# Re-ordered first loads, moved work units with filler matmuls, and head sums spread by a block matrix: a two-block transformer kernel

## The chip, the cores and the metric

The kernel runs on one core of a Trainium2 chip, as one program with its own instruction stream for each engine: TensorE (PE: matmuls), VectorE (DVE), ScalarE (ACT), GpSimd (POOL) and SyncE (SP, which here only issues DMAs). Engines meet through semaphores. The metric is the device time of the whole program in microseconds, lower is better.

## The reference

One layer of each of two blocks in float32, on 256 tokens of width 2048. Cut to what is computed:

```
mod = silu(c) @ ada_w + ada_b                       # 6 x 2048, with a table added
h = rms(x) * (1 + sc_m) + sh_m                      # block 1, mixer
xx = shift(h) - h;  x_n = h + xx * mu[n]            # six mixes: r k v w a g
r, k, v = x_r @ W_r, x_k @ W_k, x_v @ W_v
w = -softplus(-(w0 + tanh(x_w @ w1) @ w2)) - 0.5;  decay = exp(-exp(w))
a = sigmoid(a0 + (x_a @ a1) @ a2);  g = sigmoid(x_g @ g1) @ g2
kk = k * k_k, each head of 64 scaled to length 1;  k = k * (1 + (a - 1) * k_a)
y = rwkv7_scan(r, decay, k, v, -kk, kk * a)         # 32 heads of 64
y = group_norm(y) + sum(r * k * r_k) * v            # sums over each head
x = x + g_m * rms((y * g) @ w_o)
x = x + g_f * rms(conv_ffn(rms(x) * (1 + sc_f) + sh_f))   # hidden 5504
z = rms(x) @ w_in                                   # block 2: q k v g_attn, b c h g_conv
q, k = rope(rms_head(q)), rope(rms_head(k))         # 16 q heads, 4 k/v heads of 64
y1 = window_attention(q, k, v, sinks) * silu(g_attn)      # window 128, blocks of 128
y2 = b * conv3(c * h) * silu(g_conv)
x = x + [y1, y2] @ w_out
x = x + sigmoid(rms(x) @ w_gate + b) * rms(p @ w_ple)
```

## The kernel before

**Layout.** Activations lie transposed, features on the 128 partitions: 16 tiles of 128 x 256 tokens make the width of 2048. A weight unit is the 128 x 2048 slab (1 MB) that makes one output tile, in 16 matmuls. Matmuls in plain float32 (line 677 and those of the recurrence) appear in the trace as two records each. From the output projection `wo` on, each weight unit and activation is split into a rounded high part (`whi`, ScalarE, line 1227) and the rest (`wlo`, VectorE, line 1687), and a product is one matmul of high weight on both activation parts (line 700, 512 columns) and one of low weight on the high part (line 701, 256 columns).

**Loads.** SP streams the weight units through a ring of four 1 MB slots (`ring`), in the order of its program; each load waits until the unit four places ahead in the ring is used, and the loads behind it in SP's queue wait too. `RV` (line 78) is the order for projections r and v: 16 r units, then the v units with "ada" units among them. An ada unit is a row block of `ada_w`, and VectorE uses it alone, in a dot product with silu(c) over 128 x 2048 elements (`dot_into`, line 1665, `ada_ring`).

**The first stage.** SP loads x, the constants, c, the parameters, two ada blocks, the three small input matrices w1, a1, g1 of the low-rank paths, and then for each of the 16 tiles of the width a pair of ada blocks and a row block of the key matrix (`row`: 128 x 1536, four ring slots). ScalarE squares x (after silu of c), TensorE sums the squares by a matrix of ones (`rms`), ScalarE takes the root, VectorE the reciprocal (`rec`), GpSimd multiplies x by it. For tile i VectorE does two dots (`dots`) that give scale and shift, ScalarE makes h and four scaled copies, VectorE adds the shifted part (`mixes`), and TensorE adds this tile's part to 4 low-rank and 12 key outputs, held in all of PSUM. This is a loop over the contraction, so TensorE starts with tile 0 of x and not with all of h.

**The rest of the mixer.** Key tiles 12 to 15, the low-rank outputs w2 and a2, head sums of the squared keys (`sums_by_head`: stationary 64 tokens, moving a 2-column matrix that sums the two heads of a tile), r with the small triangular products and their inverse on VectorE, v with transposes of the inverse between tiles, and the recurrence in four chunks of 64 tokens. In each chunk VectorE masks eight banks of products, does some ada dots (`SCAN_DOTS`) and then copies what TensorE needs for the chunk's output. After that come eight rounds `q` of normalising: TensorE spreads the head factors over partitions (`head_spread`: stationary one broadcast column) and computes two tiles of the gate product `g2`, VectorE scales y (`y_scaled`), multiplies the bonus (`v_bonus`), GpSimd adds both, and VectorE multiplies by the gate one round later (`gated_y`), which frees the gate tile's bank.

**Attention.** In the query and key tiles of `zk` each tile's squares are summed by head into 2 columns, one root and one reciprocal are taken for all ten tiles at the end, and in the gate tiles `zg` TensorE spreads two tiles' factors at a time (`two_heads`), which VectorE multiplies in. `scores`, the softmax and `pv` then run between the tiles of `zc`.

The order of the work is written out by hand in each engine's program; nothing plans it.

## Time and profile before

| | |
|---|---|
| median of 3 runs | 2066.36 us (2059.53 to 2067.49) |
| the profiled execution | 2064.75 us, its span 2063.1 us |
| busy share of the span | PE 95%, PEld 83%, DVE 67%, ACT 43%, POOL 6% |
| matmul records | 13392 |
| mean granted TensorE clock | 0.975 of full speed |
| DMA | 419.34 MB, mean 203 GB/s |

The span runs from the first to the last instruction. PE is the matmul, PEld the weight load that runs beside it. Busy shares are averages over stages with different limits. In a timeline row, "[idle before <-releaser]" says how long the engine stood idle and whose end let it go; "issue" is idle time for which the profile shows no wait. PEclk is the clock granted to TensorE, 1.00 for 2.4 GHz and 0.50 for 1.2 GHz.

### The profile page before, as it was taken

How to read it: one execution, taken by the hardware profiler on the slowest of the kernel's cores; microseconds unless marked ns; L12 is line 12 of the kernel's file. 1: busy time of each engine (PE TensorE's matmuls, PEld its weight loads, DVE VectorE, ACT ScalarE, POOL GpSimd, SP SyncE). 2: the span in 40 equal slices, each digit the busy share in tenths (PEclk: the TensorE clock that was granted, in tenths of full speed). 3: DMA queues.
4: the chain of work that ended last, by engine and by line, in shares of the span. 5: the costliest groups of instructions: out<-in, count | busy, mean ns of one | idle time of the engine just before them, and what ended most of it. 6: DMA issues, size and time to landing. Idle time of an engine off the chain costs nothing.

```text
span 2063.1 us, 34272 instructions
## 1 busy us (share of the span) xinstructions
PE 1958.8 (95%) x13392; PEld 1703.7 (83%) x13392; DVE 1389.0 (67%) x1981; ACT 897.1 (43%) x1457; POOL 121.3 (6%) x119
## 2 busy tenths in 40 slices
PE   3999999898898988999999999999989999999999
PEld 2888888787786866888888888888878888888887
DVE  5986459643765987777777776444466567767876
ACT  2335321022233545555555555444454435535553
POOL 2000001100002310000000000000010000001200
PEclk8999999999999988999999999999999999999999
DMA  9986224565743954545555556555536444445553
GB/s 403 400 352 215 102 86 160 223 258 232 288 166 125 425 205 163 183 183 183 187 184 193 186 186 221 191 184 194 191 106 241 164 163 177 150 152 216 184 184 123
DMA packets 59078, 419.34 MB, mean 203 GB/s; under 512 B 6560, under 2 KB 6688, under 8 KB 12448
## 3 DMA queue, kind: packets, MB, share of 16 engines
q1 hardware_dynamic: 54656, 384.34, 50.3%
q0 software_dynamic: 3888, 27.26, 3.3%
q10 hardware_dynamic: 432, 6.29, 0.7%
q8 instruction: 74, 1.21, 0.2%
q14 instruction: 28, 0.23, 0.0%
HBM read 411.58 MB, written 6.29 MB: 203 GB/s over the span
## 4 chain that ended last, share of the span: by engine, by line
PE 91%; DVE 4%; DMA 2%; issue 1%; ACT 1%; SPq 0%; POOL 0%; DVEq 0%; ACTq 0%
PE ps L700 41%; PE ps L701 21%; PE ps L677 12%; PE ps L781 4%; PE ps L775 1%; PE ps L761 1%; DMA ring<-in_wv 1%; PE ps L752 1%; DMA bk<-in_ada 1%; PE ps L1007 1%; PE ps L1066 1%; PE ps L797 1%; DVE ring L1665 1%; PE ps L934 1%; PE ps L664 0%
## 5 line engine op out<-in xcount | busy, mean ns | idle before, releaser
L700 PE MATMUL ps<-x_pair,whi 128*128 128x512 f32 x2464 | 881.8, 402 | 14.4 <-DVE x_pair L1721 9.9
L701 PE MATMUL ps<-x_pair,wlo 128*128 128x256 f32 x2464 | 693.8, 282 | 0.0
L1687 DVE TENSOR_TENSOR wlo<-ring,whi 128x1024 fp32r<-128x1024 f32 x468 | 547.6, 1206 | 102.9 <-ACT whi L1227 96.5
L700 PEld LDWEIGHTS ps<-x_pair,whi 128*128 128x128 f32 x2464 | 465.2, 189 | 135.0 <-issue 21.9
L1227 ACT ACTIVATE whi<-ring 128x1024 fp32r<-128x1024 f32 x468 | 462.4, 1031 | 96.4 <-PE ps L701 93.8
L701 PEld LDWEIGHTS ps<-x_pair,wlo 128*128 128x128 f32 x2464 | 467.9, 190 | 0.3
L1234 ACT ACTIVATE px<-ps 128x256 f32<-128x256 f32 x202 | 77.8, 385 | 475.0 <-PE ps L701 475.0
L700 PE MATMUL ps<-hid_pair,whi 128*128 128x512 f32 x688 | 238.8, 394 | 0.0
L701 PE MATMUL ps<-hid_pair,wlo 128*128 128x256 f32 x688 | 190.6, 277 | 0.0
L677 PE MATMUL ps<-mixb,ring 128*128 128x256 f32 x640 | 146.6, 391 | 13.6 <-DMA ring<-in_wv 12.0
L700 PEld LDWEIGHTS ps<-hid_pair,whi 128*128 128x128 f32 x688 | 129.0, 188 | 30.2 <-DVE wlo L1687 0.3
L1665 DVE CUSTOM_DVE_ANT_0 ring<-ring,cb,prm 128x2048 f32<-128x2048 f32 x42 | 97.6, 2351 | 82.1 <-DMA ring<-in_ada 81.3
L677 PEld LDWEIGHTS ps<-mixb,ring 128*128 128x128 f32 x640 | 124.8, 196 | 33.0 <-DMA ring<-in_wv 13.1
L701 PEld LDWEIGHTS ps<-hid_pair,wlo 128*128 128x128 f32 x688 | 129.2, 188 | 0.0
L677 PE MATMUL ps<-mixa,ring 128*128 128x256 f32 x512 | 116.0, 390 | 0.0
L677 PEld LDWEIGHTS ps<-mixa,ring 128*128 128x128 f32 x512 | 99.8, 196 | 14.6 <-issue 0.2
L1750 DVE TENSOR_TENSOR px<-ps,px 128x256 f32<-128x256 f32 x68 | 28.9, 424 | 119.5 <-ACT px L1234 119.2
L1695 DVE TENSOR_TENSOR px<-ps,px 128x256 f32<-128x256 f32 x134 | 56.4, 421 | 72.1 <-ACT px L1234 71.8
L2004 DVE SCALAR_TENSOR_TENSOR tmp<-px,prm,tmp 128x255 f32<-128x255 f32 x86 | 41.6, 484 | 81.5 <-ACT tmp L1480 81.5
L700 PE MATMUL ps<-y_pair,whi 128*128 128x512 f32 x256 | 89.0, 392 | 2.5 <-DVE h L1931 1.4
L781 PE MATMUL ps<-mixb,ring 128*128 128x256 f32 x384 | 86.3, 382 | 0.0
L1480 ACT ACTIVATE tmp<-px,prm 128x256 f32<-128x256 f32 x86 | 51.8, 602 | 70.4 <-DVE px L1695 70.4
(291 smaller groups left out, 2286.3 us busy)
## 6 DMA issues: line engine op xcount, KB each, us to landing
ring<-in_fi SPq DMA_DIRECT2D x86, 1024.0 KB, 4.8
ring<-in_zin SPq DMA_DIRECT2D x52, 1024.0 KB, 4.8
ring<-in_ada SPq DMA_DIRECT2D x42, 1024.0 KB, 6.9
ring<-in_fo SPq DMA_DIRECT2D x32, 1024.0 KB, 4.8
bk<-in_ada SPq DMA_DIRECT2D x22, 1024.0 KB, 10.3
ring<-in_wr SPq DMA_DIRECT2D x16, 1024.0 KB, 4.8
ring<-in_wv SPq DMA_DIRECT2D x16, 1024.0 KB, 4.9
ring<-in_wo SPq DMA_DIRECT2D x16, 1024.0 KB, 8.9
```

The source lines that it names most:

```text
L677: last = mm(ps[0:m, bank, 0:S], w[:, k * m:(k + 1) * m], act[:, k, :], start=k == 0, stop=k == n - 1)
L700: mm(ps[:, bank, 0:2 * S], w_h, pair_k, start=first and k == 0, stop=False)
L701: m = mm(ps[:, bank, 0:S], w_l, pair_k[:, 0, :], start=False, stop=last and k == n - 1)
L781: last = mm(outer_bank(m), ring[:, i % RING, m * P:(m + 1) * P], mixb[:, i, :], start=i == 0 and m % 2 == 0, stop=i == NT - 1, skip_group_ ...
L1227: A(whi[:, hf % WB, 0:m], ring[:, u % RING, 1024 * x:1024 * x + m], ACT.Copy).then_inc(w_hi, 1)
L1234: A(part[:, (TILE[name] + k) % 4, :], ps[:, (TILE[name] + k) % BANKS, S:2 * S], ACT.Copy).then_inc(x_part, 1)
L1480: A(tmp[:, (k % 4) * S:(k % 4 + 1) * S], join_in("fi", k, it), ACT.Identity, scale=param_at("fcw", 4 * FT, kk), bias=param_at("fcb", 0, kk ...
L1665: V.tensor_tensor_reduce(out=w, in0=w, in1=cb[:], scale=1.0, scalar=prm[:, m:m + 1], op0=ALU.mult, op1=ALU.add, accum_out=mod[:, m:m + 1]) ...
L1687: V.tensor_tensor(wlo[:, hf % WB, 0:m], ring[:, u % RING, 1024 * x:1024 * x + m], whi[:, hf % WB, 0:m].bitcast(F32), ALU.subtract).then_in ...
L1695: return V.tensor_tensor(o, ps[:, (TILE[name] + k) % BANKS, 0:S], o, ALU.add).then_inc(joined, 1)
L1750: own(V.tensor_tensor(o, ps[:, (TILE[name] + k) % BANKS, 0:S], o, ALU.add))
L2004: own(V.scalar_tensor_tensor(d[:, 1:S], b[:, 0:S - 1], param_at("fcw", 2 * FT, kk), d[:, 1:S], ALU.mult, ALU.add))
```

## The change

1. First loads: x, then only the first 773 columns of the constants (the rest comes after the first stage, waited for by `ld_late`), c, parameters. The low-rank input matrices are no longer loaded ahead; their rows are appended to the key matrix's row blocks, 1984 columns instead of 1536. ScalarE squares x before it takes silu of c; VectorE takes the reciprocal before its first dots, and does tile i - 1's mixes between tile i's two dots.
2. `RV`: v0 to v5 without ada units, then two before each v tile and two behind the last. 22 dots before the recurrence instead of 24, and 4, 6, 6, 4 in its chunks instead of 5, 5, 4, 4.
3. `all_sums_by_head`: stationary 128 tokens of a tile, moving 2 columns, for two of the three uses. For it the a/r buffer `ar` is laid out tile, a/r, token, where it was tile, chunk, a/r, token.
4. `gated_y(q)` in round q.
5. `keep_clock`: n matmuls of the identity on a 256-column constant, into a bank that nothing reads: 10 and 18 around the second sum of squares (between `wo` and the FFN), 8 before `zk`.
6. Attention: the squares of a query or key tile times a block matrix of ones (`blk`) give head sums that are already spread; root on ScalarE (`head_root`), reciprocal and product on VectorE (`normalized`) for each tile. `pv` uses the first keys for both query blocks in one matmul of 256 columns. The softmax's small buffers lie over `omu`.

SP's queue at projections r and v, before and then after. in_wr and in_wv are the r and v units, in_ada the dot units:

```order
L465 DMA ring<-in_wr 128x2048 x16
L465 DMA ring<-in_wv 128x2048 x3
L465 DMA ring<-in_ada 128x2048
L465 DMA ring<-in_wv 128x2048
L465 DMA ring<-in_ada 128x2048
L465 DMA ring<-in_wv 128x2048
```

```order
L468 DMA ring<-in_wr 128x2048 x16
L468 DMA ring<-in_wv 128x2048 x6
L468 DMA ring<-in_ada 128x2048 x2
L468 DMA ring<-in_wv 128x2048
L468 DMA ring<-in_ada 128x2048 x2
```

Three more v units stand ahead of the first dot unit, and dot units then come in pairs.

VectorE's first instructions, before and then after. ISA rows are the dots and the reading of their sum, RECIPROCAL is that of the root of x's mean square, sc the scale of one tile, the rows on ar, sg and mixb the four mixes:

```order
L1771 TENSOR_TENSOR prm<-prm 128x96
L1665 ISA bk,mod<-bk,cb,prm 128x2048
L1665 ISA mod 128x1
L1665 ISA bk,mod<-bk,cb,prm 128x2048
L1665 ISA mod 128x1
L1779 SCALAR_TENSOR_TENSOR sc<-mod,prm 128x1
L1727 RECIPROCAL tmp<-tmp 128x256
L1665 ISA bk,mod<-bk,cb,prm 128x2048
```

```order
L1774 TENSOR_TENSOR prm<-prm 128x96
L1730 RECIPROCAL tmp<-tmp 128x256
L1668 ISA bk,mod<-bk,cb,prm 128x2048
L1668 ISA mod 128x1
L1668 ISA bk,mod<-bk,cb,prm 128x2048
L1668 ISA mod 128x1
L1785 SCALAR_TENSOR_TENSOR sc<-mod,prm 128x1
L1668 ISA bk,mod<-bk,cb,prm 128x2048
L1668 ISA mod 128x1
L1793 SCALAR_TENSOR_TENSOR ar<-h,prm,ar 128x255 x2
```

The reciprocal moved ahead of the first two dots, and the first mixes stand after three dots instead of four.

VectorE in the first rounds of the head normalisation, before and then after. The rows on h from ar are `y_scaled`, those on mixa `v_bonus`, those on h from h and ps `gated_y`:

```order
L1923 SCALAR_TENSOR_TENSOR h<-ar,prm,ps 128x256 x2
L1917 TENSOR_TENSOR mixa<-mixa,ps 128x512
L1923 SCALAR_TENSOR_TENSOR h<-ar,prm,ps 128x256 x2
L1917 TENSOR_TENSOR mixa<-mixa,ps 128x512
L1931 TENSOR_TENSOR h<-h,ps 128x256 x2
```

```order
L1928 SCALAR_TENSOR_TENSOR h<-ar,prm,ps 128x256 x2
L1922 TENSOR_TENSOR mixa<-mixa,ps 128x512
L1936 TENSOR_TENSOR h<-h,ps 128x256 x2
L1928 SCALAR_TENSOR_TENSOR h<-ar,prm,ps 128x256 x2
L1922 TENSOR_TENSOR mixa<-mixa,ps 128x512
```

The gate product moved up by one round, so VectorE reaches it with GpSimd's addition of the same round still to come.

The diff, cut to its core:

```diff
-    RV += [("v", _k)] + [("ada", len(RV) - NT - _k + _j) for _j in range(0 if _k < 2 else 1 if _k < 8 else 3 if _k < 10 else 2)]
-SCAN_DOTS = (5, 5, 4, 4)
-RV += [("ada", 24 + _k) for _k in range(sum(SCAN_DOTS))]
+    RV += [("v", _k)] + [("ada", len(RV) - NT - _k + _j) for _j in range(0 if _k < 5 else 2)]
+RING_DOTS = len(RV) - 2 * NT
+SCAN_DOTS = (4, 6, 6, 4)
+RV += [("ada", RING_DOTS + _k) for _k in range(sum(SCAN_DOTS))]
...
+ROW = KO * P + 2 * LORA + 2 * P
...
+    put("blk", (i // HD == j // HD).astype(np.float32))
...
-        ar = ar_f.rearrange("p (i c a t) -> p i c a t", i=NT, c=NCH, a=2)
+        ar = ar_f.rearrange("p (i a c t) -> p i c a t", i=NT, c=NCH, a=2)
+        ar_i = ar_f.rearrange("p (i a s) -> p i a s", i=NT, a=2)
...
-            sp.dma_start(cst[:], t["const"]).then_inc(ld_par, 16)
+            sp.dma_start(cst[:, 0:EARLY], t["const"][:, 0:EARLY]).then_inc(ld_cst, 16)
...
-                sp.dma_start(ring[:, i % RING, 0:KO * P], t["wkr"][i]).then_inc(ld_row[i % RING], 16)
+                sp.dma_start(ring[:, i % RING, 0:ROW], t["wkr"][i]).then_inc(ld_row[i % RING], 16)
             ada_pair(0)
-            sp.dma_start(lora_w1, t["w1"]).then_inc(ld_lora, 16)
-            sp.dma_start(lora_a1, t["a1"]).then_inc(ld_lora, 16)
-            for k in range(2):
-                sp.dma_start(flat_c[:, 2048 * k:2048 * (k + 1)], t["g1"][k]).then_inc(ld_lora, 16)
             row(0)
             for i in range(1, NT):
                 ada_pair(i)
                 row(i)
+            sp.dma_start(cst[:, EARLY:], t["const"][:, EARLY:]).then_inc(ld_late, 16)
...
+            def keep_clock(n, bank):
+                for _ in range(n):
+                    mm(ps[:, bank, 0:S], ident, const("smask"), start=True, stop=True)
...
+            def all_sums_by_head(src, bank):
+                for tt in range(TT):
+                    for i in range(NT):
+                        m = mm(ps[:, bank, tt * NH + 2 * i:tt * NH + 2 * i + 2], src(i)[:, tt * P:(tt + 1) * P], const("blk2"),
+                               start=True, stop=True)
...
-            hidden = [("w", lora_w1, LORA), ("a", lora_a1, LORA), ("g", flat_c[:, 0:2048], P), ("g", flat_c[:, 2048:4096], P)]
+            hidden = [("w", KO * P, LORA), ("a", KO * P + LORA, LORA), ("g", ROW - 2 * P, P), ("g", ROW - P, P)]
             for i in range(NT):
                 pe.wait_ge(mix_b, 4 * (i + 1))
-                for n, (name, w, m) in enumerate(hidden):
-                    last = mm(ps[0:m, n // 2, (n % 2) * S:(n % 2 + 1) * S], w[:, i * m:(i + 1) * m], mix_slot(name, i),
+                pe.wait_ge(ld_row[i % RING], 16 * (i // RING + 1))
+                for n, (name, o, m) in enumerate(hidden):
+                    last = mm(ps[0:m, n // 2, (n % 2) * S:(n % 2 + 1) * S], ring[:, i % RING, o:o + m], mix_slot(name, i),
                               start=i == 0 and n % 2 == 0, stop=i == NT - 1, skip_group_check=True)
                     if i == NT - 1:
                         last.then_inc(pe_step, 1)
-                pe.wait_ge(ld_row[i % RING], 16 * (i // RING + 1))
                 for m in range(KO):
                     last = mm(outer_bank(m), ring[:, i % RING, m * P:(m + 1) * P], mixb[:, i, :],
...
-            for c in range(NCH):
-                m = sums_by_head(c, lambda i: ar[:, i, c, 1, :], 4)
-            m.then_inc(hs_sum, 1)
+            all_sums_by_head(lambda i: ar_i[:, i, 1, :], 4).then_inc(hs_sum, 1)
...
-                    for c in range(NCH):
-                        m = sums_by_head(c, lambda i: rkr[:, i, c * CH:(c + 1) * CH], 4)
-                    m.then_inc(bon_sum, 1)
+                    all_sums_by_head(lambda i: rkr[:, i, :], 4).then_inc(bon_sum, 1)
...
             rms(1, None, NT)
+            keep_clock(10, 6)
             rms(2, mixb)
+            keep_clock(18, 6)
...
-                    m = head_sums(e)
-                    if e == 9:
-                        m.then_inc(at["sum"], 1)
+                    if e >= 2:
+                        pe.wait_ge(at["root"], e - 1)
+                    mm(ps[:, 4 + e % 2, 0:S], const("blk"), qsq[:, e, :], start=True, stop=True).then_inc(at["sum"], 1)
...
+            keep_clock(8, (TILE["zk"] + 3) % BANKS)
...
+                    pe.wait_ge(at["root"], 10)
...
-                    if e >= 2:
-                        pe.wait_ge(at["nrm"], e - 1)
-                    for tt in range(TT):
-                        m = spread_pair(rs, tt * 32 + 2 * e, 4 + e % 2, tt * P)
-                    m.then_inc(at["bc"], 1)
...
-                mm(o[:, 0:P], vtok[:, 0, kv:kv + HD], p[:, 0:P], start=True, stop=True)
-                mm(o[:, P:S], vtok[:, 0, kv:kv + HD], p[:, P:2 * P], start=True, stop=False)
-                mm(o[:, P:S], vtok[:, 1, kv:kv + HD], p[:, 2 * P:3 * P], start=False, stop=True).then_inc(at["pv"], 1)
+                mm(o[:, 0:S], vtok[:, 0, kv:kv + HD], p[:, 0:2 * P], start=True, stop=False, skip_group_check=True)
+                mm(o[:, P:S], vtok[:, 1, kv:kv + HD], p[:, 2 * P:3 * P], start=False, stop=True,
+                   skip_group_check=True).then_inc(at["pv"], 1)
...
                     one(k, None, k == n - 1)
+            act.wait_ge(ld_x, 16)
+            squares(0, mixa)
             act.wait_ge(ld_c, 16)
             A(cb[:], cb[:], ACT.Silu).then_inc(silu_c, 1)
-            act.wait_ge(ld_par, 32)
-            act.wait_ge(ld_x, 16)
-            squares(0, mixa)
...
+            def head_root(e):
+                act.wait_ge(at["sum"], e + 1)
+                A(qsq[:, e, :], ps[:, 4 + e % 2, 0:S], ACT.Sqrt, scale=1.0 / HD, bias=const("eps")[:, 0:1]).then_inc(at["root"], 1)
...
-                if k == 11:
-                    act.wait_ge(at["sum"], 1)
-                    A(rt[:].rearrange("p (a n) -> p a n", a=2)[:, :, 0:20],
-                      ps[:, 4, 0:64].rearrange("p (a n) -> p a n", a=2)[:, :, 0:20], ACT.Sqrt, scale=1.0 / HD,
-                      bias=const("eps")[:, 0:1]).then_inc(at["root"], 1)
+                for e in new_heads(k - 1):
+                    head_root(e)
...
                 for j in range(2):
                     s, m = i % 3 * 2 + j, i + NT * (1 - j)
                     dve.wait_ge(ld_ada[0][s], 16 * (i // 3 + 1))
                     dot_into(m, ada_slot(0, s))
+                    if j == 0 and i:
+                        mixes(i - 1)
...
+            rec(0)
             dve.wait_ge(silu_c, 1)
-            dots(0)
-            rec(0)
-            for i in range(1, NT):
+            for i in range(NT):
                 dots(i)
-                mixes(i - 1)
             mixes(NT - 1)
+            dve.wait_ge(ld_cst, 16)
...
-                if q in (4, 6):
-                    y_lo_part((q - 4) // 2)
+                gated_y(q)
+                if q in (2, 4, 6):
+                    y_lo_part(q // 2 - 1)
                 if q == 5:
                     lo_part("wo", 0)
-            gated_y(7)
-            y_lo_part(2)
             y_lo_part(3)
             for k in range(NT):
                 lo_part("wo", k + 1) if k < NT - 1 else lo_part("fi", 0)
...
+            def normalized(e):
+                dve.wait_ge(at["root"], e + 1)
+                own(V.reciprocal(qsq[:, e, :], qsq[:, e, :]))
+                dve.wait_ge(at["rot"], e + 1)
+                V.tensor_tensor(qk[:, e, :], qk[:, e, :], qsq[:, e, :], ALU.mult).then_inc(at["nrm"], 1)
...
-                if k == 11:
-                    dve.wait_ge(at["root"], 1)
-                    V.reciprocal(rs[:].rearrange("p (a n) -> p a n", a=2)[:, :, 0:20],
-                                 rt[:].rearrange("p (a n) -> p a n", a=2)[:, :, 0:20]).then_inc(at["rec"], 1)
...
+                if k >= 8:
+                    normalized(k - 8)
...
-                for e in two_heads(k):
-                    dve.wait_ge(at["bc"], e + 1)
-                    dve.wait_ge(at["rot"], 10)
-                    V.tensor_tensor(qk[:, e, :], qk[:, e, :], ps[:, 4 + e % 2, 0:S], ALU.mult).then_inc(at["nrm"], 1)
+                if k < 6:
+                    normalized(4 + k)
```

## Rows read from the trace of the kernel before

**Rows 1.** Page, part 4: the chain that ended last, by engine.

```profile
PE 91%; DVE 4%; DMA 2%; issue 1%; ACT 1%; SPq 0%; POOL 0%; DVEq 0%; ACTq 0%
```

**Rows 2.** TensorE's waits: what waited, on what; us in all, count, longest.

```profile
PE ps L677 <- DMA ring<-in_wv: 12.0, 4, 7.0
```

**Rows 3.** DMA issues, 0 to 170 us: size, median us from issue to landing.

```profile
mixa<-in_x SPq DMA_DIRECT2D x1, 2048.0 KB, 7.9
```

**Rows 4.** Timeline, start: start us, busy us, engine, line, operation, shape, count.

```profile
16.24 9.81 PE L664 MATMUL ps<-mixb,cst 128*128 128x256 f32 x32 [16.24 <-ACT mixb L1196]
26.60 1.75 DVE L1727 RECIPROCAL tmp<-tmp 128x256 f32<-128x256 f32 x1 [4.79 <-ACT tmp L1202]
28.44 14.09 POOL L571 TENSOR_TENSOR mixa<-mixa,tmp 128x512 f32<-128x512 f32 x8 [27.85 <-DVE tmp L1727]
...
32.31 3.20 DVE L1665 CUSTOM_DVE_ANT_0 bk<-bk,cb,prm 128x2048 f32<-128x2048 f32 x1 [3.95 <-DMA bk<-in_ada]
...
43.75 1.99 PE L775 MATMUL ps<-ar 128*96 128x256 f32 x4 [17.69 <-DVE mixb L1787]
...
156.88 27.79 PE L677 MATMUL ps<-mixb,ring 128*128 128x256 f32 x128
```

**Rows 5.** Page, part 5: costliest groups | busy, mean ns | idle before.

```profile
L1687 DVE TENSOR_TENSOR wlo<-ring,whi 128x1024 fp32r<-128x1024 f32 x468 | 547.6, 1206 | 102.9 <-ACT whi L1227 96.5
...
L1665 DVE CUSTOM_DVE_ANT_0 ring<-ring,cb,prm 128x2048 f32<-128x2048 f32 x42 | 97.6, 2351 | 82.1 <-DMA ring<-in_ada 81.3
```

**Rows 6.** Windows: PE, PEld, DVE, ACT, POOL busy (records), PEclk, DMA share, GB/s.

```profile
100.00:110.00 10.00, 10.00 (x48) 8.60 (x47) 8.95 (x14) 3.41 (x8) 0.00 (x0) 1.00 1.01 427
```

**Rows 7.** Timeline, PE, value projection.

```profile
390.51 15.64 PE L677 MATMUL ps<-mixb,ring 128*128 128x256 f32 x64 [6.97 <-DMA ring<-in_wv]
...
511.47 7.17 PE L677 MATMUL ps<-mixb,ring 128*128 128x256 f32 x32 [2.97 <-DMA ring<-in_wv]
```

**Rows 8.** Windows, PE alone, inside the key's head sums.

```profile
200.00:202.00 2.00, 2.00 (x44) 1.00 0.86 348
```

**Rows 9.** Timeline, PE: the key's head sums, and sums in an attention tile.

```profile
198.49 9.31 PE L761 MATMUL ps<-cst,ar 128*64 128x2 f32 x128
207.72 9.66 PE L677 MATMUL ps<-mixa,ring 128*128 128x256 f32 x32
...
1600.49 0.50 PE L1051 MATMUL ps<-cst,qsq 128*128 128x2 f32 x4
1600.86 0.68 PE L1090 MATMUL ps<-qk,cst 128*128 128x256 f32 x2
```

**Rows 10.** Timeline, PE, the recurrence's first chunk.

```profile
537.74 3.31 PE L984 MATMUL ps<-cum,zb 128*64 128x64 f32 x64 [2.80 <-DVE cum L1896]
```

**Rows 11.** Timeline, head normalisation rounds.

```profile
628.37 0.87 DVE L1923 SCALAR_TENSOR_TENSOR h<-ar,prm,ps 128x256 f32<-128x256 f32 x2 [2.06 <-PE ps L752]
...
643.17 1.28 POOL L599 TENSOR_TENSOR h<-h,mixa 128x512 f32<-128x512 f32 x1 [3.74 <-DVE h L1923]
643.70 0.74 DVE L1931 TENSOR_TENSOR h<-h,ps 128x256 f32<-128x256 f32 x2
644.26 1.97 PE L1007 MATMUL ps<-sg,ring 128*128 128x256 f32 x8 [1.21 <-DVE h L1931]
...
664.58 2.44 DVE L1935 TENSOR_TENSOR y_pair<-h,y_pair 128x1024 fp32r<-128x1024 f32 x2
```

**Rows 12.** Windows, PE alone, the FFN's first matmuls.

```profile
784.00:786.00 2.00, 2.00 (x7) 0.50 0.57 246
```

**Rows 13.** Timeline, ACT: outputs of two plain and two gate tiles.

```profile
1613.55 0.39 ACT L1234 ACTIVATE px<-ps 128x256 f32<-128x256 f32 x1 [3.67 <-PE ps L701]
1619.16 0.38 ACT L1234 ACTIVATE px<-ps 128x256 f32<-128x256 f32 x1 [3.02 <-PE ps L701]
...
1632.06 0.39 ACT L1234 ACTIVATE px<-ps 128x256 f32<-128x256 f32 x1 [4.29 <-PE ps L701]
1638.92 0.39 ACT L1234 ACTIVATE px<-ps 128x256 f32<-128x256 f32 x1 [4.28 <-PE ps L701]
```

76 lines of the change are left out of this document (35 added, 41 removed).

## The prediction, made before the changed kernel ran

> **What bounds the kernel now.** I read the chain of waits by engine first [rows 1]. It lies on TensorE for 91% of the span, so an edit pays only where it shortens TensorE's own work or closes a stretch in which TensorE stands still. Next I read what TensorE waits for [rows 2]: four waits on value weights, 12.0 us, are one entry, and the timeline shows them and the rest in place. The start comes first: TensorE's first tile of the first product stage begins only at 43.75 us and the stage ends at 156.88 [rows 4]. Sixteen steps in 113.1 us, the first at half clock, make 6.91 us a step. While they run the DMA engines are full too, share 1.01 at 427 GB/s [rows 6]. So this stage has two limits a few per cent apart. Later come gaps behind a transfer [rows 7], behind VectorE in the recurrence [rows 10] and in the head normalisation [rows 11], and half-clock stretches after longer pauses [rows 12].
>
> **The start.** Before, x, all constants, c and the parameters (2.10 + 0.85 + 1.05 + 0.47 = 4.47 MB) land before ScalarE squares x. Now only x is needed, the first load of all. It lands 7.9 us after its issue [rows 3], at about 9, and a quarter of the squares later, 1 us, the ones-matmuls that begin at 16.24 can begin: near 10.3. From them to GpSimd's first multiply before is 28.44 - 16.24 = 12.2 us [rows 4]; that puts GpSimd at 22.5. All of this 6 us does not reach TensorE. Before, VectorE did its first two 2.35 us dot products [rows 5] while TensorE summed. Now the reciprocal stands ahead of them in VectorE's order and they follow at 22.4, beside GpSimd's eight multiplies. Those two do not overlap: a dot takes 3.20 us while GpSimd works, and GpSimd's eight multiplies take 14.09 us [rows 4], though an operation of their shape takes 1.28 [rows 11], eight 10.2. Serial work up to the first finished mix: three dots 7.0, four mixes and the small scale 1.9, seven or eight multiplies 9.2. That is 18.3 from 22.4, so TensorE starts at 40.9 instead of 43.75, a gain of 2.8 us. The ends are -1 (a ninth slot lost, x later) and +8 (no serialising at all).
>
> The Trainium skill, "SBUF — State Buffer", section "SBUF: two separate sides", says that VectorE and GpSimd hold one port pair by an exclusive lock and the loser blocks for a whole instruction. The trace agrees: 3.20 us against 2.35. By free overlap the gain would be 8, not 2.8.
>
> Each row load grows from 1536 to 1984 columns, so a step moves 2.10 + 1.02 = 3.11 MB, 7.3 us at 427 GB/s [rows 6], against 6.91 for TensorE. The row loads run up to four steps ahead, and 0.4 us a step over the 11 steps that reuse the ring costs 4.5 us of that lead, which is about 16 (three steps less the 4.5 us of a load). I price it at nothing. VectorE's step (two dots and four mixes) keeps its length.
>
> **The value projection.** Value tile 5 waits 6.97 us and starts at half clock: two projections take 15.64 us [rows 7] where four take 27.79 [rows 4], so 1.8 more. Its load stood in SP's queue behind dot units that VectorE could not yet consume. Now values 0 to 5 come before any dot unit, and TensorE has work for those 7 us. Two more of the four waits are 12.0 - 6.97 - 2.97 = 2.06 [rows 2, 7], behind three dot units in a row; now there are never more than two, and filler work stands behind those tiles. The last wait, 2.97, stays: the same two dot units stand ahead of value 15. Gain 6.97 + 1.8 + 2.06 = 10.8. The ends are 0 (rival B) and 12.
>
> **Sums by head.** Two places go from 128 records of 64 stationary columns to 64 records of 128. In the clear stretch 44 narrow ones start in 2 us, 0.045 each [rows 8], so 128 are 5.8 us; the stretch takes 9.31 because its clock falls to half, and the next projection takes 9.66 instead of 6.93 for the same reason [rows 9]. A wide one (L1051) takes 0.37 us for four, 0.092 each or more [rows 9], so 64 are 5.9. I take nothing for both places together. If they are 0.11 and the clock falls as before they lose 1 to 1.5 each; if the clock holds, they give 3 and the slow projection's 2.7 back. Ends -3 and +11.
>
> The Trainium skill, "TensorE: Matmul & The Clock Gate", section "LDWEIGHTS (loading the stationary operand)", says a load's time goes by its columns, not its rows, so half the loads of double width gain nothing. The trace agrees, 0.045 against 0.092. By a fixed price per load the two places would gain 4.6 and 4.4, and the sum would be 9 us larger (rival A).
>
> **Recurrence dots.** Chunk 0 loses one dot of five; TensorE waited 2.80 there for the copy behind them [rows 10], so 2.35 of it goes. Chunks 1 and 2 gain one and two dots in front of their copy. Before, the copy came after the matmuls in both, so most of 2.35 and 4.7 lies in VectorE's pause; I charge 0.4 in all. Gain 1.9. Ends -3 and 2.8.
>
> **Head normalisation.** TensorE waits about 1.2 us in each round [rows 11], for a gating product that VectorE does one round after its input. The gate now stands in its own round, so VectorE waits for GpSimd's 1.28 us instead (0.6 of it under the bonus product), but the gate tiles of the next round find their bank free. A VectorE round is the scaling 0.87, the bonus product and the gate of about 0.74 each and 0.6 left of GpSimd's, 3.0 us [rows 11], plus 1.2 in every other one and 2.35 in round 5. TensorE's is 5.0 less 1.2, 3.8. So TensorE stops waiting up to round 5, then VectorE leads to the last low half, which now ends at 664.58 + 2.44 = 667.0. Counting from the first scaling at 628.37: five rounds of 3.8, then 5.2, 4.05, 2.85, and 2.4 for the last high and low halves are 33.5, so 661.9. (Rounds 2, 4 and 6 carry a low half of 1.2.) Gain 5.2. Ends 2 and 8.
>
> **Fillers.** Ahead of the FFN the clock is at 0.50, its 1.2 GHz level, when the split matmuls start [rows 12], and ahead of the attention projections likewise. A pair of 512 and 256 columns is 0.64 us there and 0.32 at 2.4 GHz. The ten fillers before the sum of squares let its last quarter run at full speed: 0.6 us. The 18 before the FFN keep the clock for its first half tile, but the second half waits for the split input either way: 0.5. The 8 before the attention projections end before its input is there, and its first eight pairs then take 2.6 instead of 5.1 us; a later wait on GpSimd's sums takes some of it: 2.0. Sum 3.1. Ends -2 (a filler stands in front of real work, or the clock falls in the rest of the pause) and 4.
>
> **Attention heads.** The spread of the normaliser leaves TensorE's gate tiles. A gate tile with two spreads takes 1638.92 - 1632.06 = 6.86 us, a plain one 1619.16 - 1613.55 = 5.61 [rows 13]. Five times 1.25 is 6.3. In the query/key tiles the wide ones-block matmul (two records, about 0.43) replaces four records at 0.37 [rows 9]: ten times 0.06, nothing to speak of. VectorE gets ten reciprocals of 1.75 us [rows 4] and a product each. A gate tile has two low halves of 1.2 [rows 5] and two short products, 3.1 us, and gets 2.2 more: 5.3 of 5.6. A query/key tile has three short products besides, 4.3, and comes to 6.5 in a tile of 5.61 + 0.37 + 0.43 = 6.4. It fits by a hair, and only the last four of those tiles have it; besides, the next low halves are wanted only after the tile that runs. If it slips, scores wait for the tenth head: up to 3. First keys for both query blocks: the same columns in fewer instructions, nothing; ends -1 and 2. Gain 6.3, ends 3 and 7.
>
> **Everything else** (the attention buffers put over the mix coefficients, the other layout of the a/r buffer, the late rest of the constants) has no duration that could change by these rows: the same elements per instruction. Ends -2 and 2.
>
> **Sum.** 2.8 + 10.8 + 0 + 1.9 + 5.2 + 3.1 + 6.3 = 30.1 us. The profiled execution took 2064.75 (span 2063.1 and 1.65 around it), 1.6 under the median of the runs, 2066.36. 2064.75 - 30.1 = 2034.7; I say 2035.
>
> **Rivals.**
> A. The sums by head get shorter in proportion and the clock stays up behind them: 9 us more, 2026. For it: half the instructions. Against it: 0.092 for a wide one [rows 9].
> B. The value gap only moves. After every value tile two dot units and the next value have to be loaded, and where nothing stands between two projections that costs 2.97 us [rows 7]. If tiles 7 to 10 meet it because VectorE frees its slots late, four times 2.97 is 11.9: 2047. Against it: sums and transposes stand between most of those tiles.
> C. Slower. The first stage goes over to the DMA queues: with 3.11 MB a step they decide as soon as a step takes longer than 6.91 us for more steps than the lead covers. To turn the sum round it needs about 9.4 us a step, 331 GB/s; then 16 steps cost 40 us and the time is about 2075. For it: share 1.01 already, nothing in reserve [rows 6]. Against it: 427 GB/s over the same queue and even longer rows.
> D. The stalls that go are taken back one for one by VectorE, which gets the reciprocals, the later dots and the wait for GpSimd: no change, 2062.
>
> **How the numbers follow.** My forecast 0.61, A 0.14, B 0.17, C 0.04, D 0.04. About 0.5%, 10 us, is what a measurement of this kernel can tell from no change. Forecast, A and B are all faster by more, except for a small part of B: faster 0.91. D and that part: 0.05. C: 0.04. The ends of the costs above, taken as independent, spread by about 12 us each way, so the range is 2022 to 2049; it holds A and B. The likeliest case alone has 2028 to 2043.
>
> **What would show it.** TensorE's first tile at 40 to 42 us and dots of over 3 us behind the reciprocal; steps of 6.9 us with no transfer wait. No wait on value weights above 1 us but the 2.97 at tile 15. 64 records of the head sums in 6 to 9.5 us each. No VectorE wait inside the normalisation rounds up to round 5, and the first split output tile near 655 less the shift. Full clock at the start of FFN and attention. Gate tiles of 5.6 to 5.7 us. It is wrong if TensorE waits for VectorE in the gate tiles, if the steps of the first stage take over 7.2 us, or if value tiles 7 to 10 wait.

## The result, and the profile after

The changed kernel takes 2044.70 us, median of 4 runs (2028.08 to 2045.49); the kernel before, with one run more on the same chip, 2064.42 (2059.53 to 2067.49). The ratio is 0.9884, 95% interval 0.9853 to 0.9916: faster by 1.2%. I forecast 2035, in 2022 to 2049. The profiled execution took 2044.51 us (span 2042.6), so the two profiles differ by 20.2 us where my sum had 30.1.

What TensorE waits for (line that waited, what let it go: us in all, times, longest), one row of the kernel before and then four of after, against [rows 2]:

```profile
PE ps L973 <- issue: 4.1, 3, 1.6
```

```profile
PE ps L680 <- DMA ring<-in_wv: 3.4, 2, 3.0
PE ps L984 <- issue: 5.7, 3, 2.1
PE ps L680 <- issue: 3.1, 1, 3.1
PE ps L703 <- DVE y_pair L1940: 3.7, 1, 3.7
```

The 12.0 us for value weights fell to 3.4. What grew has no releaser ("issue": the profile shows nothing that TensorE waits for). Such stops were there before too: four in the recurrence, 5.5 us in all, against five and 7.6 us after, and one inside value tile 14, 1.58 us against 3.14. And the wait inside `wo`'s first tile, 1.13 us before, is 3.71.

The start, timeline of after, against [rows 4]:

```profile
9.88 9.54 PE L667 MATMUL ps<-mixb,cst 128*128 128x256 f32 x32 [9.88 <-ACT mixb L1197]
21.38 1.75 DVE L1730 RECIPROCAL tmp<-tmp 128x256 f32<-128x256 f32 x1 [7.66 <-ACT tmp L1203]
23.17 3.45 DVE L1668 CUSTOM_DVE_ANT_0 bk<-bk,cb,prm 128x2048 f32<-128x2048 f32 x1
23.22 16.49 POOL L574 TENSOR_TENSOR mixa<-mixa,tmp 128x512 f32<-128x512 f32 x8 [22.63 <-DVE tmp L1730]
...
40.04 2.02 PE L791 MATMUL ps<-ar,ring 128*96 128x256 f32 x4 [20.62 <-DVE mixb L1793]
```

TensorE starts its first tile at 40.04 instead of 43.75, and GpSimd's eight multiplies now take 16.49 us instead of 14.09: three dots and four mixes of VectorE lie beside them, and not two dots and two mixes.

One more thing changed here, on ScalarE. Before it takes the root it loads another function table, 1.28 us. The row before, and then after:

```profile
18.96 1.28 ACT L1202 ACT_TABLE_LOAD   x1
```

```profile
19.51 1.28 ACT L1203 ACT_TABLE_LOAD   x1 [3.72 <-PE ps L667]
```

Before, this load lay beside TensorE's sums, and the root began at 26.10, as the sums ended at 26.05. Now silu stands between the squares and the root, the load waits for the sums, which end at 19.42, and the root begins at 20.80. So about 1.3 us of the earlier x are lost there, and no run took them back.

The value projection, timeline of TensorE, against [rows 7]:

```profile
345.42 48.51 PE L680 MATMUL ps<-mixb,ring 128*128 128x256 f32 x224
...
471.75 4.24 PE L897 MATMUL ps<-h,cum 64*32 64x32 f32 x256
...
479.98 16.17 PE L680 MATMUL ps<-mixb,ring 128*128 128x256 f32 x61 [3.14 <-issue]
...
499.12 8.86 PE L680 MATMUL ps<-mixb,ring 128*128 128x256 f32 x32 [2.97 <-DMA ring<-in_wv]
```

Seven projections run in one piece: the gap of 6.97 us is gone. But three records into value tile 14 TensorE stops for 3.14 us, and the 61 records behind the stop take 16.17 us. The kernel before, around value tiles 13 and 14:

```profile
477.13 3.14 PE L875 MATMUL ps<-cum,h 64*64 64x32 f32 x84 [1.52 <-issue]
...
496.79 11.71 PE L677 MATMUL ps<-mixb,ring 128*128 128x256 f32 x53 [1.58 <-issue]
```

There the stop in tile 14 was 1.58 us and the rest of the two projections ran at full clock. After, TensorE in the stop and behind it (us, busy (records), PEclk, DMA share, GB/s):

```profile
476.00:480.00 4.00, 0.86 (x4) 0.87 1.02 420
480.00:484.00 4.00, 4.00 (x10) 0.50 0.23 94
```

From the start of value tile 14 to the recurrence it is 32.58 us instead of 26.59 (from 475.92 and 492.57), 6.0 us lost: the longer stop, half clock behind it, and half clock behind the wait at tile 15. Ahead of tile 14 other things got shorter: the stop of 1.52 us at 477.13 became one of 0.31 and value tile 13 behind it ran at full clock, 2.8 us together, and the two small waits for value weights gave 1.7.

A round of the head normalisation and the second half of `wo`'s first tile, against [rows 11]:

```profile
624.28 0.75 DVE L1936 TENSOR_TENSOR h<-h,ps 128x256 f32<-128x256 f32 x2 [0.70 <-POOL h L602]
625.84 0.87 DVE L1928 SCALAR_TENSOR_TENSOR h<-ar,prm,ps 128x256 f32<-128x256 f32 x2 [0.81 <-PE ps L755]
626.72 0.69 DVE L1922 TENSOR_TENSOR mixa<-mixa,ps 128x512 f32<-128x512 f32 x1
```

```profile
645.54 0.49 PE L703 MATMUL ps<-y_pair,whi 128*128 128x512 f32 x1 [1.51 <-DVE h L1936]
652.29 0.49 PE L703 MATMUL ps<-y_pair,whi 128*128 128x512 f32 x1 [3.71 <-DVE y_pair L1940]
```

VectorE is now the one that waits in a round (0.70 and 0.81 us), and the rounds start 3.82 us apart.

The ledger below is made of the start of the same instruction in both traces. Its last column is the difference within the stretch.

| stretch | before | after | gained |
|---|---|---|---|
| to the key's head sums | 198.49 | 194.79 | 3.7 |
| key's head sums and the next projection | 18.83 | 19.11 | -0.3 |
| value projection up to the bonus sums | 57.24 | 48.34 | 8.9 |
| bonus sums and two projections | 25.79 | 25.98 | -0.2 |
| from there to the recurrence | 87.29 | 88.76 | -1.5 |
| recurrence | 106.15 | 106.64 | -0.5 |
| normalisation to the second half of `wo`'s first tile | 41.85 | 37.15 | 4.7 |
| from there to `wo`'s first output | 3.07 | 4.64 | -1.6 |
| last `wo` output to second FFN output | 44.58 | 43.63 | 0.9 |
| FFN output matrix, 15 tiles | 223.60 | 227.89 | -4.3 |
| last FFN output to first `zk` output | 28.33 | 25.78 | 2.6 |
| the rest of the `zk` tiles | 79.11 | 79.90 | -0.8 |
| gate tiles 0 to 7 | 46.99 | 40.99 | 6.0 |
| the last 34 outputs (`zo` and `pg`) | 194.17 | 191.58 | 2.6 |
| what is left: fi and `zc` | 687.80 | 687.65 | 0.2 |

The rows come to 20.5, the difference of the spans. Two of them belong to no edit: in the FFN's output matrix and in the last projections the same matmuls run at another pace.

### The profile page after: what moved, and what is told of

The parts are those of the page before. It is cut to its first block, busy times and chain, and to the rows that moved or that the text cites. A ratio compares the mean times of both kernels' runs of the same rounds, so it can differ in the third digit from the quotient of the medians.

```text
span 2042.6 us, 33937 instructions
## 1 busy us (share of the span) xinstructions
PE 1967.2 (96%) x13204; PEld 1710.0 (84%) x13204; DVE 1409.8 (69%) x1990; ACT 902.8 (44%) x1467; POOL 124.5 (6%) x119
## 4 chain that ended last, share of the span: by engine, by line
PE 90%; DVE 5%; issue 2%; DMA 2%; ACT 1%; POOL 1%; SPq 0%; DVEq 0%; POOLq 0%; ACTq 0%
PE ps L703 42%; PE ps L704 21%; PE ps L680 12%; PE ps L796 4%; PE ps L791 1%; DVE ring L1668 1%; PE ps L776 1%; DMA ring<-in_wv 1%; PE ps L812 1%; PE ps L1073 1%; PE ps L667 1%; PE ps L769 1%; POOL h L602 0%; DVE bk L1668 0%; DVE mixb L1895 0%
## 5 line engine op out<-in xcount | busy, mean ns | idle before, releaser
L703 PE MATMUL ps<-hid_pair,whi 128*128 128x512 f32 x688 | 243.3, 399 | 0.0
L703 PEld LDWEIGHTS ps<-hid_pair,whi 128*128 128x128 f32 x688 | 129.3, 188 | 32.4 <-DVE wlo L1690 0.3
L2006 DVE SCALAR_TENSOR_TENSOR tmp<-px,prm,tmp 128x255 f32<-128x255 f32 x86 | 41.6, 484 | 81.5 <-ACT tmp L1482 81.5
```

Source lines behind the costliest of these rows:

```text
L703: mm(ps[:, bank, 0:2 * S], w_h, pair_k, start=first and k == 0, stop=False)
L2006: own(V.scalar_tensor_tensor(d[:, 1:S], b[:, 0:S - 1], param_at("fcw", 2 * FT, kk), d[:, 1:S], ALU.mult, ALU.add))
```

## The pace of a matmul pair, and why runs differ

Outputs of the FFN's output matrix (43 pairs of a 512 and a 256 column matmul in each tile), after, and then the same kernel in another execution:

```profile
1304.44 0.38 ACT L1235 ACTIVATE px<-ps 128x256 f32<-128x256 f32 x1 [2.13 <-PE ps L704]
1319.62 0.39 ACT L1235 ACTIVATE px<-ps 128x256 f32<-128x256 f32 x1 [2.11 <-PE ps L704]
```

```profile
1294.26 0.39 ACT L1235 ACTIVATE px<-ps 128x256 f32<-128x256 f32 x1 [2.04 <-PE ps L704]
1309.16 0.38 ACT L1235 ACTIVATE px<-ps 128x256 f32<-128x256 f32 x1 [2.04 <-PE ps L704]
```

15.18 us a tile, and 14.90: 353 and 347 ns a pair, at granted clock 1.00 in both. The second is from this experiment, which changes nothing:

> The changed kernel once more, unchanged, to learn what differs between executions. Its four times were 2044.5, 2045.5, 2028.1 and 2044.9 us, and in its profiled execution TensorE takes 5.55 us for a tile of the output projection wo, 5.65 for one of the FFN's fi, 15.19 for one of fo, 5.55 for most of the last projection zo; the kernel before had 5.55, 5.65, 14.91 and 5.65, with the same matmuls and no waits. Theory P (the pace of a matmul pair takes one of two values, 347 or 353 ns, by execution and not by code): the times again spread over more than 8 us with values near both 2028 and 2045, and this profile can show other paces in fi, fo or zo than the first one, at unchanged start (TensorE's first tile at 40.0 +-0.5 us). Theory Q (the pace belongs to the program's code): the same paces stage by stage, 5.55, 5.65, 15.19, 5.55, and the one time of 2028 stays alone.

Measured: 2041.50 us, median of 6 (2032.44 to 2045.66), ratio 0.990 [0.9883, 0.9916] to 17 runs of the kernel before. In its profile fi's tiles take 5.55 us (5.65 in the first profile of the same kernel), fo's 14.91 (15.19), and the last projections begin at 5.55 and end at 5.65; the first tile starts at 40.73, 0.2 past the bound I had set. Theory P holds: two values and nothing between them. Over the fourteen profiles each of `wo`, fi and fo shows both (`wo` 5.55 or 5.65), and within the last projections the pace can change behind a tile that took 0.4 us longer. fi alone has 85 intervals, 9 us between the two, fo 16 tiles, 4.5. The profiles of after and of its repeat are 12.1 us apart, and these two stages alone make 13 of it. The four runs of the changed kernel spread over 17 us; the ones without a trace cannot be split up like this, so that the pace explains their spread too is likely and not shown. What selects the pace is open. For the experiments it means that a stretch of the trace decides, and the whole time only over several runs.

## The experiments

**Dots ahead of the reciprocal.**

```diff
-            rec(0)
             dve.wait_ge(silu_c, 1)
-            for i in range(NT):
+            dots(0)
+            rec(0)
+            for i in range(1, NT):
                 dots(i)
```

> The changed kernel with VectorE's first two dots ahead of the first reciprocal again, as in the kernel before; all else of the new start stays. Theory S (VectorE and GpSimd take turns, so dots done before GpSimd starts are not lengthened and don't lengthen GpSimd's eight multiplies): the two dots run at about 15.9 to 20.6 us at 2.35 each, the reciprocal still at 21.4, GpSimd at 23.2, and behind the reciprocal only one dot of about 3.4 and four mixes stand before TensorE's first tile: 23.2 + 3.4 + 5.8 = 32.4, against 40.0. The first stage then ends up to 7 us earlier, about 146 to 149, and the whole is 2037 to 2041 at the same pace of matmuls. Theory M (the DMA queues take over, 3.11 MB a step at 420 GB/s is 7.4 us): TensorE starts at 32 to 34 but the stage still ends at 151 to 153, with waits of TensorE for ring or of VectorE for bk. Theory N (the order made no difference): first tile at 39 to 41.

Measured: 2035.91 us (2029.83 to 2038.84, 4 runs), 0.9873 [0.9853, 0.9892]. Its timeline:

```profile
16.09 2.35 DVE L1668 CUSTOM_DVE_ANT_0 bk<-bk,cb,prm 128x2048 f32<-128x2048 f32 x1 [2.22 <-ACT cb L1295]
...
21.72 1.75 DVE L1730 RECIPROCAL tmp<-tmp 128x256 f32<-128x256 f32 x1 [0.78 <-ACT tmp L1203]
23.50 3.45 DVE L1668 CUSTOM_DVE_ANT_0 bk<-bk,cb,prm 128x2048 f32<-128x2048 f32 x1
23.55 13.40 POOL L574 TENSOR_TENSOR mixa<-mixa,tmp 128x512 f32<-128x512 f32 x7 [22.96 <-DVE tmp L1730]
...
32.61 2.02 PE L791 MATMUL ps<-ar,ring 128*96 128x256 f32 x4 [12.78 <-DVE mixb L1793]
```

TensorE starts at 32.61, where theory S had 32.4. The two dots fit into VectorE's idle time while TensorE sums, and the ones beside GpSimd are the long ones (3.45 us against 2.35; a mix 1.48 against 0.48). The key sums start at 187.21, 7.6 us earlier, so theory M falls too: 3.11 MB a step did not hold the stage. TensorE starts 11.1 us earlier than in the kernel before, where the change as made has 3.7: its order gave back two thirds of what the new first loads had opened. Of the 7.6 us, 3.5 are left at the recurrence: this run lost 1.6 in the key sums and the projection behind them, where the clock fell earlier, and 2.5 in the value tiles to half clock and stops.

**Without the fillers.**

```diff
-            keep_clock(10, 6)
...
-            keep_clock(18, 6)
...
-            keep_clock(8, (TILE["zk"] + 3) % BANKS)
```

> The changed kernel without the 10, 18 and 8 filler matmuls. Theory F (they pay by keeping the clock up): the stretch from the sum of squares behind wo to the second FFN tile's output is 0.9 to 1.2 us longer than the 40.65 us of the changed kernel (743.11 to 783.76), and the stretch from the sum of squares behind fo to the first zk output 2.0 to 2.6 longer than 23.23 (1504.49 to 1527.72), with the granted clock at 0.50 in the first FFN and zk matmuls; in all 3 to 3.8 us. Theory G (the time there went otherwise, by an earlier x_lo or another order): both stretches within 0.3 us of the changed kernel's.

Measured: 2044.64 us (2042.51 to 2047.65, 4 runs). Ahead of `zk` theory F holds: from the sum of squares to the first `zk` output 25.71 us against 23.23, and from the last FFN output 28.25 against 25.78 in after and 26.23 in its repeat. TensorE's clock in the first `zk` matmuls (us, busy (records), PEclk, DMA share, GB/s), without fillers and then with them:

```profile
1516.50:1518.50 2.00, 2.00 (x8) 0.50 0.00 0
```

```profile
1518.00:1520.00 2.00, 1.66 (x9) 1.00 0.04 8
```

How much the 8 fillers buy is less sure than these rows say. From the last FFN output to the first `zk` output the eleven traces with them have 25.8 to 26.3 us; the three without them have 28.3, 28.3 and 27.3 (the last in the run with the gate's place alone, below). So it is between 1.0 and 2.6 us.

Ahead of the FFN it is theory G: from the sum of squares to the second fi output 41.04 us without fillers and 40.65 in after, but 41.44 in its repeat and 41.44 in the run with the dots first, all three with fillers. Over all traces it is 40.7 to 42.0 with fillers and 40.7 to 41.6 without. The 28 fillers there buy nothing that shows: in the repeat the first half tile runs at full clock and TensorE then waits for the split input of the second half:

```profile
773.08 0.49 PE L703 MATMUL ps<-x_pair,whi 128*128 128x512 f32 x1 [2.09 <-DVE x_pair L1724]
```

The 0.9 us in the ledger is scatter.

**All dots early.**

```diff
-SCAN_DOTS = (4, 6, 6, 4)
+SCAN_DOTS = (10, 10, 0, 0)
```

> The changed kernel with the dots of the recurrence's four chunks as 10, 10, 0, 0 instead of 4, 6, 6, 4. TensorE's stops inside the chunks for which the trace shows no wait (1.0 to 2.1 us each, in the middle of a run of 64 small matmuls, at DMA share 1.0) are 7.6 us in all in the changed kernel. Theory I (TensorE's own instruction stream comes late there because the dot units' transfers, which VectorE now frees, fill the DMA engines): no such stop in chunks 2 and 3, where no load runs but at most the first four of wo, so chunk 2 takes 23.5 to 24.2 us instead of 25.3 and the last one is 1.5 to 2 shorter. The first two chunks get longer by VectorE: ten dots are 23.5 us, so they are 14 and 9 us longer. Theory J (the stops are the small matmuls' own): the stops stay at 1 to 2 us in chunks 2 and 3 as well.

Measured: 2060.78 us (2055.85 to 2066.84, 10 runs), as costly as the first two chunks said (36.4 and 37.0 us). The third chunk of four took 21.9 us instead of 25.3 and the last stretch 26.2 instead of 32.2. All of TensorE's waits there (578 to 631 us), and three of those in after over the whole recurrence (508 to 615), beside the 5.7 us on line 984 shown above:

```profile
PE ps L769 <- ACT ar L1416: 0.3, 1, 0.3
PE ps L995 <- DVE cum L1901: 0.2, 1, 0.2
```

```profile
PE ps L995 <- issue: 1.9, 2, 1.2
PE ps L995 <- DVE cum L1901: 1.4, 3, 0.7
PE ps L984 <- ACT cum L1409: 1.2, 1, 1.2
```

No stop without a name is left. The clock also fell later in the head sums at the recurrence's end. Here they begin at 618.24, in after at 598.18. The stretch from about 2 to 4 us into them, here and then in after:

```profile
620.00:622.00 2.00, 2.00 (x45) 1.00 0.00 0
...
624.00:626.00 2.00, 2.00 (x43) 0.50 0.00 0
```

```profile
600.00:602.00 2.00, 2.00 (x24) 0.50 0.16 61
```

The first 60 sums took 3.3 us instead of 5.9, but the clock came down to 0.50 here too, as the second row shows.

But both the transfers and VectorE's dots were gone from those chunks. The next run parts them.

**Dots without their loads.**

```diff
+                if name == "ada" and k >= RING_DOTS:
+                    sp.sem_inc(landed[u % RING], 16)
+                else:
                     load(u, ...)
```

> The changed kernel without the loads of the 20 dot units that stand beside the recurrence. VectorE does the same dots on what the slots hold, so those 20 columns of mod are wrong and only the transfers are gone. In the experiment with the dots early, chunks without loads and without dots took 21.9 us, against 25.3 with both, and the last one 26.2 against 30.6 to 32.9. Theory I (the transfers hold up TensorE's instruction stream): the chunks are 19.5 to 20, 22 to 23 and 22 to 23 us from one spread of its masks to the next, the last 26 to 28, and no stop without a named wait is over 0.5 us except where wo's first loads run. Theory V (VectorE's dots do it, through memory or semaphores): the chunks stay at 24.5 to 25.5 us with stops of 1 to 2 us.

Measured: 2039.71 us (2036.66 to 2046.79, 4 runs). The chunks take 20.8, 23.8, 24.3 and the last 29.2. TensorE's waits (508 to 611 us):

```profile
PE ps L998 <- DVE cum L1904: 5.0, 3, 2.7
PE ps L987 <- issue: 1.3, 1, 1.3
PE ps L987 <- ACT cum L1412: 1.2, 1, 1.2
```

The stops go, but for the one of 1.3 us where the loads of the gate matrix and of `wo` run, so in the recurrence it is the transfers (theory I) and not VectorE's dots that stop TensorE between small matmuls. No run took away the loads beside value tile 14, so for the stop there this is a likeness and not shown. The sizes I gave for the chunks were wrong all the same: with the loads gone VectorE's six dots are late, 2.13 and 2.67 us. The second and third chunks without these waits are 21.7 us each, as in the run before. That is why moving a dot is worth so little: the loads of a chunk cost TensorE stops of 1.7 to 3.3 us together in after, and where the stops end VectorE's copy is next. The expectation's theory I also says what is held up, TensorE's own instructions. That fits the rows (in after DMA share 0.94 to 1.07 during the stops in the recurrence and 1.02 in the one of 3.14, right behind a dense burst of 256 instructions in 4.24 us), but no run shows the instructions themselves, and it stays a reading. A full share is not needed the whole time either: the kernel before stopped for 1.46 us with a mean share of 0.59 (564.4 to 565.9).

**The gate's place alone**, in the kernel before.

```diff
-                if q:
-                    gated_y(q - 1)
+                gated_y(q)
```

> The kernel before with the gate product moved into its own round, and nothing else of the change. Theory H (this move alone closes TensorE's stops in the normalisation rounds): from the first gate tile's matmuls to the second half of wo's first tile 37 to 37.5 us, as in the changed kernel (615.14 to 652.29), instead of 41.85 before (625.31 to 667.16); then a wait of about 3.7 us inside wo's first tile, half clock behind it, and so 3 us net at wo's first output. Theory K (the stops went because other parts of the change gave VectorE room): 40 to 42 us and waits of 1.1 to 1.3 us for h in each round.

Measured: 37.15 us (624.43 to 661.58), exactly the changed kernel's; it includes the last wait, of 3.70 us, and from there to `wo`'s first output it is 4.46 us. Theory H. 2056.40 us (2051.16 to 2069.10, 10 runs), 0.9974 [0.9949, 1.0000].

**Narrow sums again.** The same at the bonus place.

```diff
-            all_sums_by_head(lambda i: ar_i[:, i, 1, :], 4).then_inc(hs_sum, 1)
+            for c in range(NCH):
+                m = sums_by_head(c, lambda i: ar[:, i, c, 1, :], 4)
+            m.then_inc(hs_sum, 1)
```

> The changed kernel with the old sums by head (128 matmuls of 64 stationary columns) at both places, from the new layout. In the changed kernel a wide one takes 0.10 us at full clock and 0.18 at half, a narrow one before 0.048 and 0.08; the stretch of sums and the next projection is 19.1 us at the key place (194.79 to 213.90) and 26.0 at the bonus place (393.76 to 419.74, two projections). Theory W (the price goes by columns, and the clock falls in both): 18.4 to 19.6 and 25.4 to 26.6 us, the whole within 1 us at equal pace. Theory X (the wide form is worth having): over 1 us longer at each place.

Measured: 18.9 us at the key place and 25.7 at the bonus place; 2036.10 us (2029.03 to 2042.75, 4 runs). Theory W: the wide form gains nothing, and costs 0.2 to 0.3 us more at each place. The key place of after:

```profile
194.80:196.80 2.00, 2.00 (x20) 1.00 0.35 70
...
200.80:202.80 2.00, 2.00 (x11) 0.50 0.00 0
```

0.10 us a wide matmul, 0.18 when the clock has fallen, against 0.045 to 0.05 and 0.08 for a narrow one, so half as many of twice the columns cost the same.

**The old order of the units**, the rest of the change kept.

```diff
-    ... for _j in range(0 if _k < 5 else 2)]
+    ... for _j in range(0 if _k < 2 else 1 if _k < 8 else 3 if _k < 10 else 2)]
...
-SCAN_DOTS = (4, 6, 6, 4)
+SCAN_DOTS = (5, 5, 4, 4)
```

> The changed kernel with the old order of r, value and dot units and the old split of dots over the recurrence (24, then 5, 5, 4, 4). Theory R (the order alone made the value gap): TensorE waits 6.9 to 7.0 us for value unit 5 again, with half clock behind it, so from the end of r's sums to the bonus sums 8.5 to 9.2 us longer than 189.35 (204.41 to 393.76); the stop without a named wait at value tile 14 about 1.6 instead of 3.1 and no half clock behind it; the recurrence's first chunk 23 to 24.6 instead of 19.7 to 20.8, the third 23.7 to 24.1 instead of 24.8 to 25.6, so that the four are within 2 us of the changed kernel's. In all 7 to 11 us more at the same pace. Theory T (the new first loads had already made room): the gap is 5 us or less.

Measured: 2055.38 us (2051.39 to 2063.64, 10 runs), 0.9960 [0.9941, 0.9979]. The wait of 6.89 us is back:

```profile
PE ps L680 <- DMA ring<-in_wv: 11.8, 4, 6.9
PE ps L680 <- issue: 3.1, 1, 3.1
```

From the end of the key sums to the bonus sums 197.3 us, 8.0 more than after (8.5 to 9.2 expected), and to the recurrence 317.0, 12.9 more. So the order is worth 13 us when it alone is undone, where the ledger shows 7.2 for that region (the kernel before, with the same old order, takes 311.4 from the end of the key sums to the recurrence, 5.6 less than this run). The expectation missed the second line: the stop at value tile 14 is 3.1 us with the old order too, with half clock behind it. It was 1.6 and 1.8 in the two profiles of kernels that begin as before, and 2.3 to 4.4 in all that have the new start. Which part of the change brings it is open.

**Three edits together**: dots first, units 14 and 15 behind 13 with three dot units behind 8 to 11, and `y_scaled(7)` ahead of `gated_y(6)`.

```diff
-    ... for _j in range(0 if _k < 5 else 2)]
+    ... for _j in range(0 if _k < 5 or _k in (13, 14) else 3 if 8 <= _k < 12 else 2)]
```

> The changed kernel with three edits in separate places: VectorE's first two dots ahead of the reciprocal (as in the second experiment, where TensorE started at 32.6 us); the value units 14 and 15 loaded right behind 13, with three dot units instead of two behind 8 to 11; and the last scaling of y ahead of the last but one gate product. By the theory of the transfers in TensorE's way: no wait of 2.97 us at value tile 15, and from the bonus sums' end to the recurrence (104.2 us, 404.29 to 508.50, in the changed kernel) 99 to 102; the stop of 3.1 us at value tile 14 stays or moves, since some load always runs there. The wait inside wo's first tile 2.0 to 2.6 instead of 3.7. In all 2027 to 2036 as the pace falls out, 8 to 13 us less than the changed kernel at the same pace. By the rival (VectorE cannot take three dots in a tile): new waits for value units 9 to 12, each over 1 us, and nothing gained there: 2032 to 2041.

Measured: 2030.86 us (2019.33 to 2039.26, 6 runs), 0.9846 [0.9810, 0.9881]. First tile at 31.65; the wait at value 15 gone, but 3.54 us for value 9 in its place and 104.3 us from the end of the bonus sums to the recurrence, as in after: the rival in the expectation. The wait in `wo`'s first tile 1.91 us, and with it no half clock: from the first gate tile to `wo`'s first output 38.5 us instead of 41.8.

**Fillers in the sums**, with three dot units behind 9 to 12.

```diff
                     for i in range(NT):
+                        if i % 4 == 3:
+                            keep_clock(1, 7)
```

> The combined version, with value units 9 to 12 and not 8 to 11 followed by three dot units, and one filler (identity on 256 columns, two records) after every third of the 64 head sums at both places. At 2.4 GHz 16 fillers cost 16 x 0.21 = 3.4 us and 64 sums 6.4 us. Theory L (what lets the clock fall is how few columns the sums move, and the fillers keep it up): granted clock 1.0 through both places, 9.8 us each for sums and fillers, and the projections behind them at 6.93 us each instead of 9.5 and 8.5: from 194.79 to 213.90 it was 19.1 us and becomes 16.8; at the bonus place 26.0 becomes 23.8. Theory O (too few): the clock still falls, and both places are 3 to 5 us longer than before. The wait for value unit 9 of the combined version (3.54 us) goes or gets under 1.5 us, as the units behind which it stood come one tile later. In all about 2022 to 2032.

Measured: 2034.32 us (2021.10 to 2040.94, 6 runs). Theory O: the key place is 25.9 us instead of 19.1.

```profile
190.00:193.00 3.00, 3.00 (x16) 0.58 0.48 202
193.00:196.00 3.00, 3.00 (x13) 0.50 0.00 0
```

With one matmul of 256 columns for every four sums the clock fell all the same, and the bonus place was 29.5 us instead of 26.0. (The expectation says "after every third"; the code puts one ahead of every fourth.) The wait for value 9 is gone.

**The combined version** is that without the fillers in the sums. Against the first combined version:

```diff
-    ... else 3 if 8 <= _k < 12 else 2)]
+    ... else 3 if 9 <= _k < 13 else 2)]
```

> The combined version with value units 9 to 12 followed by three dot units and without fillers in the head sums. Taken together from the two runs before it: TensorE's first tile at 31.6 us, key sums at 187, no wait over 1 us for value units, the wait inside wo's first tile 1.9, and from the end of the bonus sums to the recurrence 100 to 102.5 us (104.3 in the first combined version, 102.0 with the fillers). The rival is that the value stage only trades one stop for another: a stop without a named wait of 3 us or more with half clock behind it, and 104 again. In all 2020 to 2030 at the faster pace of fi, up to 2038 at the slower one, median about 2028.

Measured: 2024.44 us (2019.92 to 2027.95, 6 runs), 0.9824 [0.9791, 0.9858]; value waits 1.9 us in all, none over 1.0; the stop at value tile 14 is 2.57; and 103.8 us from the end of the bonus sums to the recurrence, past what I expected: the rival's trade of one stop for another is mostly right. Its median is 20 us under the changed kernel's, the lowest of all with the next run's. But the kernel before was faster beside it too (2061.41), and the ratios, 0.9824 against 0.9884 and 0.9900 for the changed kernel and its repeat, are 12 to 16 us apart. The traces say less: this one is 18.7 us shorter than after's, but 13 of that are fi and fo at the faster pace, so about 6 are left for the edits. Its recurrence took 109.5 us, 2.8 more than in after, with unnamed stops of up to 2.67 us.

**Sums in two pieces**, in the combined version; `halves` picks 128 of the 256 tokens.

```diff
                     pe.wait_ge(bonp, 1)
-                    all_sums_by_head(lambda i: rkr[:, i, :], 4).then_inc(bon_sum, 1)
+                    all_sums_by_head(lambda i: rkr[:, i, :], 4, (0,))
+                elif k == 7:
+                    all_sums_by_head(lambda i: rkr[:, i, :], 4, (1,)).then_inc(bon_sum, 1)
```

> The same, with the 64 sums of the bonus place cut into 32 behind value tile 6 and 32 behind value tile 7. The clock fell about 4 us into every run of sums so far (at 198.8 us for sums from 194.8, at about 397 for sums from 393.8), and 32 sums at 0.10 us are 3.2 us. Theory L2 (a short run of light work does not bring the clock down): granted clock 1.0 through both pieces, 3.2 us each, and value tiles 7 and 8 at 7.1 us each, so from the start of the bonus sums to the first transpose behind tile 8 20.6 to 21.2 us instead of 26.0. Theory O2 (the light work adds up, or each piece is enough): the clock falls in one of them or behind it, and it is 23 to 27 us. In all 5 us less than the version above at the same pace under L2.

Measured: 2024.62 us (2016.66 to 2035.70, 6 runs), no gain over 2024.44. Theory O2: from the first sum to the first transpose 28.2 us, against 27.7 in one piece. The clock behind each piece:

```profile
388.00:392.00 4.00, 3.37 (x19) 0.65 0.98 389
392.00:396.00 4.00, 4.00 (x11) 0.50 1.01 422
...
404.00:408.00 4.00, 4.00 (x11) 0.50 1.00 422
```

It was 1.00 at the start of each piece and 0.50 in the projection behind it, twice. (The expectation's first words on the clock, "about 4 us into every run of sums", do not hold for all runs: with the dots first the sums begin at 187.21, and from 189 to 191 the clock is already 0.62 in the mean.)

## Why the prediction was right, and 10 us too large

**The start** (2.8): 3.7. The mechanism was right, dots of 3.45 us beside GpSimd, and TensorE began at 40.04 where I had 40.9 (my terms add up to 22.4 + 18.3 = 40.7). In part two errors cancelled: from the first ones-matmul to GpSimd it took 13.3 us and not 12.2, by the table load, and from GpSimd's start to TensorE's first tile 16.8 and not 18.3. What I did not ask is why the dots had to follow the reciprocal; the answer was worth 7.6 us.

**The value projection** (10.8): 7.4 in the ledger. The gap with its half clock gave 8.9 against 8.8, the two small waits 1.7 against 2.06, the wait at 15 stayed at 2.97. The failed step is what I left out. The sum has no term for stops without a releaser, though the trace before has two here: the one in value tile 14 grew from 1.58 to 3.14 and with the half clock of two tiles cost 6.0 us, the one ahead of tile 13 shrank and gave 2.8, so 3.2 us net.

**Sums by head** (0, ends -3 and 11): -0.5, which is what the narrow form gave back. Rival A fell by the measured 0.10.

**Recurrence** (1.9, ends -3 and 2.8): -0.5. Chunk 0 gained 3.4 between the spreads of its masks (23.1 to 19.7), more than the dot's 2.35. Chunks 1 and 2, charged 0.4, lost 1.7, and the last stretch 2.2. I had counted only VectorE's time; each dot also brings a load, and these stop TensorE. From one trace to the next this scatters by more than the edit is worth: over the nine profiles with the new split the four stretches come to 99.8 to 105.7 us, mean 101.9, over the three with the old one to 101.8 to 104.2, mean 102.8. Chunk 0 is shorter in all nine, the sum is not clear of the scatter.

**Head normalisation** (5.2): 3.1. The rounds gave 4.7, and the gate's place alone is all of it. The part I missed lies behind: with one last wait of 3.71 us instead of several short ones the clock fell, -1.6, a term I had nowhere. In the four traces where that wait was 1.9 us the clock held, and both together were 3.3 us shorter.

**Fillers** (3.1): 1.0 to 2.6 ahead of `zk` where I said 2.0, and nothing that shows ahead of the FFN where I said 1.1. (A pair of matmuls at full clock is 0.347 us or more in the traces, not my 0.32.)

**Attention heads** (6.3): 5.2. The gate tiles gave 6.0:

```profile
1619.30 0.38 ACT L1235 ACTIVATE px<-ps 128x256 f32<-128x256 f32 x1 [3.07 <-PE ps L704]
1624.94 0.39 ACT L1235 ACTIVATE px<-ps 128x256 f32<-128x256 f32 x1 [3.07 <-PE ps L704]
```

5.64 us against 6.86 in [rows 13], and VectorE is busy for 5.20 us of that stretch, 5.3 forecast. The query/key tiles took 0.8 back, 0.09 each, where I had 0.06 and called it nothing. No run took this edit away alone; the rows of the stretch itself are the evidence.

**Pace and rest**: -1.5, by chance. Rival B fell because no value tile from 7 to 10 waited over 0.42 us, C because the stage, started 7.4 us earlier in the run with the dots first, still ran at 420 GB/s with no wait for a transfer on TensorE, D because the stalls of the rounds and the gate tiles went for good.

So the sum was 10 us too large against these two traces, 8 at equal pace. The range of 27 us held it, though the draw of the pace alone moves a trace by 13. Nearly all of the 8 is one kind of error: every stall that goes was counted in full, and none of the stalls that come was. Three came: the longer stop at value tile 14 (3.2 net), what came up in the recurrence (2.4 under the forecast), the clock inside `wo` (1.6).

## What to carry to other kernels

When a stall is removed, look in the trace for stops that no engine explains, in dense runs of small matmuls beside loads. Give them a term, and one for the clock behind them: here they stayed, and one of them doubled. Before an operation is put ahead of others to start an engine sooner, ask what will run beside that engine and whether idle time ahead of it would have held the others. And where the runs of one kernel scatter more than the effect, compare stretches of traces from the same instruction to the same instruction, and repeat the unchanged kernel once.

## What I had not expected of the hardware

- A pair of 512 and 256 column matmuls with their weight loads takes 347 or 353 ns at full clock, for whole stages, by execution: 13 us in this kernel's FFN alone.
- Loads beside dense small matmuls stopped TensorE for 0.7 to 2.7 us at a time with no releaser, mostly at DMA share 0.94 to 1.07. Without loads and dots a chunk of the recurrence took 21.9 us instead of 25.3; with the dots and without the loads 23.8 and 24.3, of which 2.13 and 2.67 were waits for VectorE.
- The granted clock went from 1.00 to 0.50 in or behind the two-column matmuls at the key and bonus places in every form tried: narrow, wide, with fillers, in two pieces. At the recurrence's end it fell as well, but later in the two runs without loads in the chunks: there the first 60 sums took 3.3 us, elsewhere 3.9 to 6.0.
- VectorE's mixes beside GpSimd took 1.48 us instead of 0.48, its dots 3.45 instead of 2.35: about 1 us more for each instruction, at either length.
